# Attention: the scores of two steps issued together, four banks for scores and two for turned rows

## The reference

```
q = (rmsnorm(c_q, g_q) @ w_uq)    # 8 heads, 128 + 64 (rotary) wide
kv = (rmsnorm(c_kv, g_kv) @ w_ukv)
def block(qn, qr, i):             # 128 queries, i = 0..3
    s = (qn @ k_nope.T + qr @ k_rope.T) * scale
    s = where(key_chunk <= q_chunk, s, -inf)   # chunks of 64
    p = softmax(s)
    return p @ v
o = concat(block(...)) @ w_o
```

## Time and profile before

| | |
|---|---|
| median of 3 runs | 1110.53 us (1110.17 to 1111.12) |
| the profiled execution: its time | 1110.07 us |
| its span, first to last instruction | 1108.3 us |
| PE busy | 1097.8 us, 99% |
| DVE, ACT busy | 783.7 us (71%), 481.8 us (43%) |
| granted TensorE clock, mean | 0.998 |

### The profile page before, as it was taken

One profiled execution on the slowest core, in us unless ns is written; L12 is line 12 of the kernel. 1 busy time (PEld: TensorE's weight loads), 2 busy tenths in 40 slices (PEclk: granted clock), 3 DMA queues, 4 the chain that ended last, 5 costly groups with the idle time before them and its releaser, 6 DMA issues.

```text
span 1108.3 us, 15338 instructions
## 1 busy us (share of the span) xinstructions
PE 1097.8 (99%) x5904; PEld 907.2 (82%) x5904; DVE 783.7 (71%) x1172; ACT 481.8 (43%) x738; POOL 63.7 (6%) x162
## 2 busy tenths in 40 slices
PE   9999999999999999999999999999999999999997
PEld 6778878888888888888888888888888888888886
DVE  6869848688777888978858866547673477635674
ACT  7557734454334443344542334334442244413453
POOL 1383031000000000000000000000000000000000
PEclk9999999999999999999999999999999999999999
DMA  7332213223243332333378743222223222222222
GB/s 233 112 118 70 68 50 122 87 104 133 97 151 114 108 121 99 129 115 119 123 243 259 219 124 101 89 95 98 107 81 114 95 96 95 94 96 96 93 83 91
DMA packets 66216, 128.60 MB, mean 116 GB/s; under 512 B 22432, under 2 KB 34464, under 8 KB 66144
## 3 DMA queue, kind: packets, MB, share of 16 engines
q1 hardware_dynamic: 64848, 123.30, 33.7%
q0 software_dynamic: 1152, 4.19, 1.1%
q10 hardware_dynamic: 144, 0.13, 0.0%
HBM read 110.50 MB, written 14.88 MB: 113 GB/s over the span
## 4 chain that ended last, share of the span: by engine, by line
PE 94%; DVE 3%; DVEq 1%; ACT 1%; issue 1%; DMA 0%; ACTq 0%
PE bank L1691 28%; PE bank L1692 28%; PE bank L1693 28%; PE bank L1897 2%; PE bank L2048 1%; PE bank L1882 1%; PE bank L1961 1%; PE bank L2037 1%; PE bank L1763 1%; PE bank L2024 0%; PE bank L1869 0%; PE bank L1870 0%; PE bank L1872 0%; PE bank L1871 0%; DVE WL L967 0%
## 5 line engine op out<-in xcount | busy, mean ns | idle before, releaser
L577 ACT ACTIVATE WH<-RAW 128x1024 fp32r<-128x1024 f32 (+1 forms) x178 | 183.7, 1033 | 371.2 <-PE bank L1693 351.1
L1691 PE MATMUL bank<-GH,WH 128*128 128x512 f32 x816 | 320.8, 393 | 0.0
L1693 PE MATMUL bank<-GH,WL 128*128 128x512 f32 x816 | 317.7, 389 | 0.0
L1692 PE MATMUL bank<-GL,WH 128*128 128x512 f32 x816 | 317.6, 389 | 0.0
L967 DVE TENSOR_TENSOR WL<-RAW,WH 128x1024 fp32r<-128x1024 f32 (+1 forms) x178 | 211.8, 1190 | 39.0 <-ACT WH L577 38.3
L1691 PE MATMUL bank<-AH,WH 128*128 128x512 f32 x570 | 223.5, 392 | 0.9 <-DVE RAWR L1144 0.8
L1693 PE MATMUL bank<-AH,WL 128*128 128x512 f32 x570 | 222.0, 389 | 0.0
L1692 PE MATMUL bank<-AL,WH 128*128 128x512 f32 x570 | 221.8, 389 | 0.0
L1691 PEld LDWEIGHTS bank<-GH,WH 128*128 128x128 f32 x816 | 153.2, 188 | 32.9 <-issue 0.8
L1693 PEld LDWEIGHTS bank<-GH,WL 128*128 128x128 f32 x816 | 153.2, 188 | 32.2
L1692 PEld LDWEIGHTS bank<-GL,WH 128*128 128x128 f32 x816 | 153.3, 188 | 31.7 <-issue 0.7
(11 more groups left out here) (296 smaller groups left out, 1020.2 us busy)
## 6 DMA issues: line engine op xcount, KB each, us to landing
RAW<-in_w_up SPq DMA_DIRECT2D x88, 512.0 KB, 3.2
RAW<-in_w_dn SPq DMA_DIRECT2D x32, 512.0 KB, 3.2
RAW<-in_w_glu SPq DMA_DIRECT2D x16, 512.0 KB, 3.3
RAW<-in_w_dn SPq DMA_DIRECT2D x16, 384.0 KB, 3.0
RAW<-in_w_wo SPq DMA_DIRECT2D x8, 512.0 KB, 3.3
od_scratch<-OO SPq DMA_DIRECT2D x8, 512.0 KB, 3.3
kd_scratch<-KT SPq DMA_DIRECT2D x8, 512.0 KB, 4.5
O<-od_scratch POOLq DMA_DIRECT2D x8, 512.0 KB, 5.4
```

What stands on the lines that cost most here:

```text
L577: act_(w_hi(b)[:, :n], RAW[b % RW][:, :n], ACT.Copy).then_inc(s_hi, 1)
L1691: mm(out, wh, hi_[:, k, :], start=start, stop=False)
L1692: mm(out, wh, lo_[:, k, :], start=False, stop=False)
L1693: return mm(out, wl, hi_[:, k, :], start=False, stop=stop)
```

## The change

The banks are dealt anew: scores go to `bank[2 + n % 4]` (four), turned rows to `bank[6 + n % 2]` (two). So `scores(n)` now waits for `exps(n - 4)`, where it was `exps(n - 3)`; `turn(n)` waits for `pt_copy(n - 2)`, where it was `pt_copy(n - 3)`. The PE loop goes over pairs: `scores(n)`, `scores(n + 1)`, then `turn(n - 3)`, `turn(n - 2)`, then one half of `pv`. What ACT, DVE and SP issue, and in which order, is the same, but for the banks' numbers. In the tail three heads of output block 0 are issued ahead of `turn(29)` and `pv(6)`; the first two output blocks take banks 2 and 3, where it was 4 and 7.

```diff
-        return (4, 7)[i]
+        return (2, 3)[i]
...
-                act_(PR_[qb][:, :N], bank[2 + n % 3][:, :N], ACT.Exp, bias=MX[:, n:n + 1],
+                act_(PR_[qb][:, :N], bank[2 + n % 4][:, :N], ACT.Exp, bias=MX[:, n:n + 1],
...
-                     bank[5 + n % 3][:, 0:(qb + 1) * P].rearrange("p (a b) -> p a b", a=qb + 1),
+                     bank[6 + n % 2][:, 0:(qb + 1) * P].rearrange("p (a b) -> p a b", a=qb + 1),
...
-                if n >= 3:
-                    pe.wait_ge(s_p, n - 2)
+                if n >= 4:
+                    pe.wait_ge(s_p, n - 3)
...
+                if n == 3:
+                    pe.wait_ge(s_read["kq"], UNIT_READ[21][1])
...
             def turn(n):
                 qb = n % 4
-                if n == 0:
-                    pe.wait_ge(s_read["kq"], UNIT_READ[21][1])
                 pe.wait_ge(s_pn, n + 1)
-                if n >= 3:
-                    pe.wait_ge(s_ptc, n - 2)
+                if n >= 2:
+                    pe.wait_ge(s_ptc, n - 1)
                 for kb in range(qb + 1):
-                    m = nc.tensor.transpose(bank[5 + n % 3][:, kb * P:(kb + 1) * P],
+                    m = nc.tensor.transpose(bank[6 + n % 2][:, kb * P:(kb + 1) * P],
...
-            for n in range(4 * HEADS):
-                scores(n)
-                if n in UNIT_IN:
-                    project(UNIT_IN[n])
-                if n >= 3:
-                    turn(n - 3)
-                if n >= 8 and n % 4 < 2:
-                    pv(n // 4 - 2, ((0, 2), (1, 3))[n % 4])
+            for n in range(0, 4 * HEADS, 2):
+                for m in (n, n + 1):
+                    scores(m)
+                    if m in UNIT_IN:
+                        project(UNIT_IN[m])
+                for m in (n - 3, n - 2):
+                    if m >= 0:
+                        turn(m)
+                if n >= 8:
+                    pv(n // 4 - 2, ((0, 2), (1, 3))[n % 4 // 2])
...
+            pe.wait_ge(s_lo, WO + 1)
+            pe.wait_ge(s_p, 4 * HEADS - 3)
+            heads(0, range(0, 3))
             turn(4 * HEADS - 3)
             pv(HEADS - 2, range(TT))
-            pe.wait_ge(s_lo, WO + 1)
-            pe.wait_ge(s_p, 4 * HEADS - 2)
-            heads(0, range(0, 6))
+            heads(0, range(3, 6))
             turn(4 * HEADS - 2)
             turn(4 * HEADS - 1)
             pe.wait_ge(s_lo, WO + 2)
-            pe.wait_ge(s_ptc, 4 * HEADS - 2)
+            pe.wait_ge(s_p, 4 * HEADS - 2)
             heads(1, range(0, 6))
```

More of the change, by code:

```diff
@@ L1180, in row_max @@
                 if n < 4:
-                    v.memset(bank[2 + n % 3][0:CHUNK, N - CHUNK:N], NEG)
+                    v.memset(bank[2 + n % 4][0:CHUNK, N - CHUNK:N], NEG)
                     v.drain()
-                v.tensor_reduce(MX[:, n:n + 1], bank[2 + n % 3][:, :N], AX.X, ALU.max, negate=True).then_inc(s_mx, 1)
+                v.tensor_reduce(MX[:, n:n + 1], bank[2 + n % 4][:, :N], AX.X, ALU.max, negate=True).then_inc(s_mx, 1)
             def normalize(n):
@@ L1866, in scores @@
                 qs = slice(qb * P, (qb + 1) * P)
-                out = bank[2 + n % 3][:, :N]
+                out = bank[2 + n % 4][:, :N]
                 mm(out, QH[:, h, qs], KH[:, h, :N], start=True, stop=False)
```

## The result

| | before | changed |
|---|---|---|
| median of 20 runs | 1110.80 us (1109.37 to 1111.12) | 1112.32 us (1111.13 to 1113.40) |
| ratio, 95% interval | | 1.0015 (1.0009 to 1.0022) |
| the profiled execution: time, span | 1110.07, 1108.3 us | 1112.30, 1110.5 us |
| attention, first scores to the end of `pv(7)`, in the trace | 85.35 to 153.57: 68.22 us | 85.08 to 155.70: 70.62 us |

The changed kernel is slower by 0.15%, 1.5 us in the medians. The forecast was 1111.9 us, 1.4 over the median that was known then.

A forecast was written before the change was run, and what follows sets the result against it. PE, busy 99% of the span, was taken as the bound; turn 6's wait 1.2, its load 0.1 and later turns 0.5, less 0.36 removed, gave +1.4 us: 1111.9 us. The 8-in-10 range was 1110.3 to 1113.9.

The forecast's parts named there:

- Removed waits: PE's waits for copies of turned rows ahead of `pv(0)` and `pv(6)` go: -0.2 and -0.16, together -0.36 us.
- More room for scores: `scores(n)` waiting for `exps(n - 4)` wins nothing, as no row shows PE waiting for `exps` before.
- Turn 6: Head 1's third turn, due at 102.5, waits on PE for turn 4's copy, ended 103.71: 1.2 us, bounds 0.7 to 1.4.
- The five later turns: Turns 10, 14, 18, 22, 26: bank free about when due, a tie; 0.1 us each, +0.5, bounds 0 and 0.5 each.
- rival A: Every head waits, the copy's chain outlasting PE's 2.87 us by 0.3 or more: +3.5 us, 1114.0; chance 0.18.
- The cost of an unhidden weight load: A waiting matmul's weight load on PE isn't hidden: 0.1 us more for turn 6, within the later five's 0.1 each.
- Switching costs nothing: On PE, changing between scores, turns and `pv` costs nothing; the slots of a 6.44 us head add up.
- Rival C: Bunching pays: four fewer changes between scores and turns per head; at 0.12 us each, -2.4 us, 1108.1; chance 0.04.
- Where scores 28 would start: Sign: scores 28 start about 1.5 us later than 133.44, but for 0.79 of `pv` put ahead of them.
- The clock: PE's granted clock, 1.00 in the attention stretch, was expected to stay; anything under 9 in its row would be wrong.
- rival D: Bunched turns let PE's clock fall to 1.2 GHz for one head, 6.4 us more: 1118; chance 0.02.
- The sum: All terms, 1.2 + 0.1 + 0.5 - 0.36 = +1.4 us: profiled execution 1111.5, median 1111.9.

The follow-up runs named there:

- experiment 1: Changed kernel's paired order with the banks and waits of before (three for scores, three for turned rows): 1110.20 us, ratio 0.9997 to the kernel before.
- Experiment 3: Changed kernel with the second turn of each pair moved behind the half of `pv`: 1110.24 us, ratio 0.9998 to the kernel before.
- experiment 6: Changed kernel with ACT's `o_hi` behind the next head's first copy and step 7's rotary copy behind turn 4's: 1110.66 us, 1.0002 to the kernel before.
- experiment 5: Changed kernel with a single bank for turned rows, `turn(n)` waiting for `pt_copy(n - 1)`: 1125.88 us, ratio 1.0139 to the kernel before.
- experiment 2: Kernel before, its loop and tail kept, with the change's banks and waits (four and two): 1111.04 us, ratio 1.0004 to the kernel before.

## Why the prediction was right

**Removed waits: right.** 0.36 us was forecast; both entries are gone, 0.40 us of weight load.

**More room for scores: right.** Nothing gained; experiment 1 has no wait of scores with three banks either.

**Turn 6: right in place, cause and size.** Forecast: due at 102.5, copy ended at 103.71, 1.2 us and 0.1 for the load. Found: due at about 102.4, copy ended at 103.64, so 1.23 us of wait, and 1.43 in all. Experiment 3 moved the turn and experiment 6 the copy, and both took most of it away.

**The five later turns: right cause, size too small.** Forecast 0.5 us in all, found 1.18. Take turn 10, with E = 107.47, the end of the 512-wide scores' slot in the trace. The sum said: due at E + 2.87, bank free at E + 2.8. It was due at 110.02 + 0.24 = E + 2.79; the copy ended at E + 2.88, and the load began 0.12 after that, not 0.03. Three errors of about 0.1 us, all to one side, of a difference between two sums of 2.8 us. The copy's came from DVE, whose row maximum began at E + 0.73 where the sum said E + 0.61:

```profile
108.20 0.68 DVE L1183 TENSOR_REDUCE MX<-bank 128x1 f32<-128x512 f32 x1
```

"A tie" was a fair reading, but the tie fell to rival A's side: every later head waits. From one 128-wide scores to the next the later heads take 6.71, 6.59, 6.81 and 6.62 us, 6.68 on average, and "over 6.6 us (A)" was named as a sign of being wrong. Only A's price, 0.5 us a head, was not reached: an average of 0.24 us each, nearer to A's threshold than to the 0.1 chosen.

**The cost of an unhidden weight load: right in kind, too small.** 0.1 us was put on it for turn 6; 1.43 less the wait of 1.23 leaves 0.20. Of that 0.11 lies between the end of the copy and the start of the load.

**Switching costs nothing: right.** Experiment 1, 6.45 us a head against 6.44. Rival C, which needed over 0.1 us for each change of kind, is refuted.

**Where scores 28 would start: a misreading.** The sign given was 1.5 us later than 133.44, but for 0.79 of `pv` put ahead of them. Nothing more stands ahead of them in the new order than in the old: the same turns up to 24 and both halves of `pv(4)`. They start at 135.53, 2.1 us later, and waits of turns are nearly all of it.

**The clock: right.** 1.00 in the stretch, with five turns in a bunch (0.55 us), so rival D is refuted here. Its rule of the Trainium skill ("TensorE: Matmul & The Clock Gate", "Part 4: PE-mode transpose"), that transposes don't count the way matmuls do, has no visible effect in bunches this short beside matmuls; no run shows longer ones.

**The sum.** +1.4 forecast; +1.5 by the medians, +2.4 by the two attention stretches. That the medians come so near is partly luck. The sum was made for the profiled execution, 1111.5 us, and that one took 1112.30: 0.8 too little, of which the five later turns are 0.7. By the traces its terms sum to 2.2, close to the upper end that the forecast had given a chance of 0.05 (turn 6 at 1.4, the heads at 0.25 each: 1.43 and 0.24 were found); the medians look nearer because the profiled execution of before was 0.7 us faster than its median.

## What to carry to other kernels

A bank taken from one ring and given to another is judged by which of the two is ever waited for: here no step waited for a bank of scores, and with one more of them and one fewer for turned rows the second ring became the bound. When calls are moved forward in an order, ask for each what it must find free, and follow on the other engine what stands ahead of the instruction that frees it: here a 0.28 us copy was late because of a 0.63 us one that belonged to something else. On PE, busy 99% of the time here, the new order alone gave nothing (experiment 1); it could only take away or bring waits. And where two engines' sums of nearly 3 us come out as a tie, as at the five later turns, each error of 0.1 us counts once for every time around the loop.

## What the hardware showed unexpectedly

A turn's weight load begins 0.11 to 0.12 us after the end of the copy that it waits for, each time: 103.64 to 103.75, 110.35 to 110.47, 116.95 to 117.06 in the changed kernel, 115.32 to 115.44 in experiment 5, 101.95 to 102.06 in experiment 2. For `pv(0)` it was 0.04 (102.03 to 102.07). ACT follows DVE's row maximum by 0.04 too (108.88 to 108.92 in the changed kernel). The waits of experiment 2 and of `pv(0)` are PE's for the same ACT instruction, the copy of turn 3; what makes the difference was not tried.
